# Start addresses of a float32r kernel's split operands in SBUF: transposed rows 16 bytes down, gated columns 16 bytes up

## The reference, cut to what matters

```
q = (xb @ w_query)...; s = einsum('thpc,pkc->thpk', q, sub_keys)   # 8 heads, 2 x 128 keys
... top_k twice -> expert indices e, gates g
act = gelu(einsum('td,thkd->thk', xb, expert_u[e]))
out = einsum('thk,thkd->td', g * act, expert_v[e])
```

## Time and profile before

| what | value |
|---|---|
| median of 2 runs | 1329.14 us (1326.47 to 1331.81) |
| the profiled execution, device time | 1329.18 us |
| its span, first to last instruction | 1327.3 us |
| PE busy / weight loads busy | 1268.4 us / 1212.0 us |
| DVE / ACT / POOL busy | 727.5 / 676.5 / 669.5 us |
| mean granted PE clock | 0.981 of 2.4 GHz |

### The profile page before, as it was taken

One profiled execution on the slowest core, in us unless ns is written; L12 is line 12 of the kernel. 1 busy time (PEld: TensorE's weight loads), 2 busy tenths in 40 slices (PEclk: granted clock), 3 DMA queues, 4 the chain that ended last, 5 costly groups with the idle time before them and its releaser, 6 DMA issues.

```text
span 1327.3 us, 26744 instructions
## 1 busy us (share of the span) xinstructions
PE 1268.4 (96%) x9917; PEld 1212.0 (91%) x9917; DVE 727.5 (55%) x1494; ACT 676.5 (51%) x1202; POOL 669.5 (50%) x286
## 2 busy tenths in 40 slices
PE   7988999898999999999999999999999999799996
PEld 5876999898999999999999999999999987699875
DVE  2444149994066666775666656666537632346423
ACT  4555444444566655555554455544544564346552
POOL 6735769999866666663000000000047765567653
PEclk9989999999999999999999999999989999899999
DMA  5724545455544444445666655666564433444432
GB/s 210 259 88 140 193 143 186 162 176 174 193 152 145 142 145 143 144 143 190 191 192 195 195 192 190 192 196 195 178 220 147 140 128 127 156 131 150 142 121 80
DMA packets 59141, 218.59 MB, mean 165 GB/s; under 512 B 6656, under 2 KB 6696, under 8 KB 58688
## 3 DMA queue, kind: packets, MB, share of 16 engines
q1 hardware_dynamic: 56592, 206.07, 47.1%
q0 software_dynamic: 1792, 8.95, 1.8%
q10 hardware_dynamic: 688, 2.62, 0.5%
HBM read 215.50 MB, written 4.21 MB: 166 GB/s over the span
## 4 chain that ended last, share of the span: by engine, by line
PE 82%; issue 7%; POOL 7%; DVE 2%; ACT 2%; DMA 0%; POOLq 0%; DVEq 0%; ACTq 0%
PE A L503 27%; PE W L503 18%; POOL ringl L460 5%; PE A L527 5%; PE A L528 5%; PE A L532 4%; PE W L765 4%; PE A L547 4%; PE A L549 4%; PE A L554 4%; POOL ringl L424 1%; PE W L581 1%; PE W L928 1%; PE W L899 1%; PE W L640 1%
## 5 line engine op out<-in xcount | busy, mean ns | idle before, releaser
L424 POOL TENSOR_TENSOR ringl<-ring,ringh 128x1024 fp32r<-128x1024 f32 x137 | 338.0, 2482 | 183.2 <-ACT ringh L976 176.7
L460 POOL TENSOR_TENSOR ringl<-ring,ringh 128x1024 fp32r<-128x1024 f32 x126 | 321.2, 2555 | 102.6 <-ACT ringh L1136 78.6
L503 PE MATMUL W<-XTh,ringh 128*128 128x256 f32 x1024 | 291.5, 285 | 8.2 <-POOL ringl L460 8.1
L503 PE MATMUL W<-XTl,ringh 128*128 128x256 f32 x1024 | 285.1, 278 | 0.0
L503 PE MATMUL W<-XTh,ringl 128*128 128x256 f32 x1024 | 285.1, 278 | 0.0
L503 PE MATMUL A<-Hh,ringh 128*128 128x256 f32 x1024 | 283.2, 277 | 0.0
L503 PE MATMUL A<-Hl,ringh 128*128 128x256 f32 x1024 | 283.1, 276 | 0.0
L503 PE MATMUL A<-Hh,ringl 128*128 128x256 f32 x1024 | 283.0, 276 | 0.0
L976 ACT ACTIVATE ringh<-ring 128x1024 fp32r<-128x1024 f32 x135 | 142.0, 1057 | 157.3 <-PE A L532 71.2
L503 PEld LDWEIGHTS W<-XTh,ringh 128*128 128x128 f32 x1024 | 194.0, 189 | 10.2 <-issue 9.8
L1136 ACT ACTIVATE ringh<-ring 128x1024 fp32r<-128x1024 f32 x189 | 197.4, 1045 | 0.4 <-DMA ring<-exp_v 0.4
(11 more groups left out here) (263 smaller groups left out, 2108.4 us busy)
## 6 DMA issues: line engine op xcount, KB each, us to landing
ring<-exp_u SPq DMA_DIRECT2D x128, 512.0 KB, 3.2
ring<-exp_v SPq DMA_DIRECT2D x128, 512.0 KB, 3.6
ring<-w SPq DMA_DIRECT2D x72, 512.0 KB, 3.2
ring<-w_out SPq DMA_DIRECT2D x24, 512.0 KB, 3.2
ring<-w_in SPq DMA_DIRECT2D x20, 512.0 KB, 3.4
ring<-w_query SPq DMA_DIRECT2D x16, 512.0 KB, 3.2
skewed<-scratch POOLq DMA_DIRECT2D x1, 2048.0 KB, 11.4
H<-lng POOLq DMA_DIRECT2D x2, 1024.0 KB, 6.7
```

The costliest lines, as they stand in the source:

```text
L424: pool.tensor_tensor(ringl[:, slot, :], ring[:, slot, :], ringh[:, slot, :].bitcast(F32), ALU.subtract)\
L460: pool.tensor_tensor(ringl[:, slot, :], ring[:, slot, :], ringh[:, slot, :].bitcast(F32), ALU.subtract)\
L503: last = pe.matmul(dst, stationary[a], moving[b], start=start and n == 0, stop=stop and n == 2, skip_group_check=True)
```

## The change

It moves tiles in SBUF and nothing else. `XTh`, `XTl`, `Hh` and `Hl` get four numbers (16 bytes) that are not used ahead of their data, and each of the four now has a home of its own. The tiles' data begin at 161,456 and 170,160 (`XTh`, `XTl`: 176 modulo 512) and at 222,416 and 224,976 (`Hh`, `Hl`: 208 modulo 512). The ring begins at 181,504, 193,792 and 206,080, which is 512 higher and again 256 modulo 512. So in products with `XTh`/`XTl` the operand from the ring begins 80 bytes above the other one, in products with `Hh`/`Hl` 48 bytes, where it was 64 in both. What lies between (`gain`, `RB`, `GF`, `bias_s`, `w_idx2`, `stat`, `PICKT` and others) moves by 512 bytes, and `WI`, `zeros`, `primer` and `m8` behind `Hl` by 1,056. The instructions of all five engines, their order, their shapes and their waits are the same as before; only line numbers move by two.

```diff
-        home(192)
-        XTh = sb("XTh", [P, KC, T], F32R)
-        XTl = sb("XTl", [P, KC, T], F32R)
+        home(160)
+        XTh = sb("XTh", [P, 4 + KC * T], F32R)[:, 4:].rearrange("p (c t) -> p c t", c=KC)
+        home(160)
+        XTl = sb("XTl", [P, 4 + KC * T], F32R)[:, 4:].rearrange("p (c t) -> p c t", c=KC)
...
         home(192)
-        Hh = sb("Hh", [P, 2, T], F32R)
-        Hl = sb("Hl", [P, 2, T], F32R)
+        Hh = sb("Hh", [P, 4 + 2 * T], F32R)[:, 4:].rearrange("p (c t) -> p c t", c=2)
+        home(192)
+        Hl = sb("Hl", [P, 4 + 2 * T], F32R)[:, 4:].rearrange("p (c t) -> p c t", c=2)
```

## The result

The changed kernel takes 1359.65 us (median of 2 runs, 1358.82 to 1360.49) against 1329.14 before: a ratio of 1.0234 with a 95% interval of 1.0195 to 1.0273. It is 30.5 us slower. The forecast of no change failed, and so did its range, which ended at 1346.

The account below looks back on a forecast made before the run. The prediction took PE's pace from one float32r matmul to the next as the bound. Its terms, 0 + 0 + 0 + 0 against the profiled 1329.18 us, gave a forecast of 1329 us, range 1317 to 1346.

Parts of the forecast that it names:

- the floor of 111.3 ns: Shortest time between matmul starts, set by loading 128 stationary columns; read where matmuls have only 8 or 16 moving numbers.
- Rival 2: Every product with a moved operand gets slow, at 48 and 80 alike: 29.9 us more, 1359 us; 7 in 100.
- the part by part: The prediction's walk through unused bytes, writing engines, `Hh`/`Hl`, and `XTh`/`XTl` as moving and stationary operand, each taken as 0.
- the quick pace: 113.4 ns for a matmul with 256 moving numbers, throughout the down stage and in parts of the up stage.
- the slow pace: 117.8 ns for the same matmul, 4.4 ns more, in parts of the up stage; 13.5 us for the down stage.
- Rivals 3 and 4: `XTh`/`XTl` lose the slow pace, 10.2 us less, 10 in 100; all reach the load's floor, 26.0 us less, 5 in 100.
- rival 1: The down stage locks into the slow pace from its start: 13.5 us more, 1343 us; 20 in 100.
- Rival 5: The change does nothing, since reads of the two operands never touch each other at any distance: 1329 us; 13 in 100.

Follow-up runs that it names:

- h48_only: Changed kernel with `XTh` and `XTl` back at distance 64, `Hh` and `Hl` still at 48: 1344.84 us, ratio 1.0111.
- all_up_16: Kernel before with `XTh`, `XTl`, `Hh`, `Hl`, `ringh`, `ringl` all 16 bytes higher, distance still 64: 1319.61 us once; timed again 1321.82 us, ratio 0.9953.

## Why the prediction was wrong

**Right.** The pace of float32r matmuls on PE was the only thing at stake; ACT, DVE and POOL were busy for as long as before, within 2.5 us, and the order was the same. The lower bound held: no stage came down to the floor of 111.3 ns. So did the reading that PE keeps the pace it meets after a wait until the next one. Rival 2 named what happened, and gave nearly the right total.

**The step that failed** stands twice in the part by part: "I take the quick pace as before, 0, since it is the row of the same instruction", and for `XTh`/`XTl` "I take 0: both paces remain, in about the present shares". The rows of before were all taken at one distance, and the forecast used them for two others. Off 64 modulo 256 the quick pace was not met at all: of thirteen other distances (0, 16, 32, 48, 68, 72, 80, 96, 112, 128, 160, 192 and 224 modulo 256), each read in one stage or both, not one had it. In the changed kernel both kinds of product ran at about 119.2 ns instead. The two paces seen at one set of addresses were read as a sign that both would remain at any other. They were a sign only that one placement can have two.

**The chance that failed** is that of rival 2, "`XTh` and `Hh` move in opposite directions, so one cause that harms both is less likely than one". That would hold on a slope. Around a narrow good place a step to either side is a step off it, and 48 (119.2 ns) and 80 (60.37 / 504 = 119.8 with its start, 119.3 from start to start) cost the same.

**The sizes.** "Above, the nearest row is the slow pace" was no bound. The new pace of 119.2 cost the down stage 17.9 us, not 13.5. Ahead of it 9.8 us were lost, where all of the up stage and the columns stages were put at 12.8: PE's idle time in the first half of the up stage, 187 - 178.80 = 8.2 us before, is down to 6.5 in the same window after, so part of the slower pace went into waits that PE had anyway. The last part lost 2.0, less than its scatter: it took 359.4 us in h48_only, with `XTh`, `XTl` and the ring at the addresses of before. The rows stages, put at 3.6 us under rival 2, went from 229.2 to 230.1 ns a matmul from start to start, 0.8 us over 912. Rival 2's sum of 29.9 against the measured 30.5 is thus two errors that cancel: 4.4 us too little for the down stage, 4.6 too much for the rest. Rivals 3 and 4 had nothing for them at these distances (all_up_16 did lose the slow pace, but by moving both operands); rival 1's pace did not come up in the traced down stages at 64.

One reading of the prediction is off without touching its sum: the up and the down stage, 186 to 963 us, are 777 of 1327 us, 59%, not two thirds.

**The rule.** Rival 5 goes with the rule cited in the prediction: the Trainium skill (TensorE: Matmul & The Clock Gate, Part 2, on the weight load) says that the moving operand and the weights are read through two independent ports. Here the measurement decides against taking it to mean that their addresses do not matter: with the same instructions, 334.78 us at a distance of 64 and 351.98 at 48. The runs show that the two operands' distance counts. They do not show where inside the chip the two reads meet, or whether it is the two reads that meet, nor why the same paces come back after 256 bytes.

## What to carry to other kernels

Where PE runs float32r matmuls without a break, the start of the moving operand against that of the stationary one is a tuning number that was worth 3 to 6% of such a stage here, and 2.3% of the kernel. Sweep it over 256 bytes on the chip, in steps small enough: 4 bytes lost the quick pace here. Look at the piece of the chain of the stage in question: the down stages at 64 and 320 agreed within 0.04 us from trace to trace, where whole executions of before scattered by 9 us and once by 20. Move both together before blaming one tile's place. A pace read at one placement does not bound what another has, on either side, even where the rows show two paces for one instruction.

## What the runs showed of the hardware that was not expected

- A matmul with 256 moving float32r numbers and a load of 128 columns takes 113.4 ns at a distance of 64 or 320 bytes (at the quick pace), and 116.7 to 120.1 ns at every other distance that was tried in the down stage. Pairs 256 apart agree within 0.01 us in 335 to 350 us.
- 4 bytes are enough to lose the quick pace: at 68 a stretch of 504 matmuls took 60.05 us, at 64 57.40.
- At 64 there is a second pace of 117.8 ns. PE falls into it after some waits and keeps it until the next one: 25 us at a time in before, 57 us in h48_only with the same addresses, every other unit where gates lie between. With the parts 16 or 48 bytes higher it was nowhere in the three traced up stages, and 16 higher made the kernel 0.5% faster (0.9934 to 0.9971).
